# x loaded ahead of everything by tile, constants made early, passes on the identity before x is scaled, and a split signal in the sample rounds

## The reference

```
h = rms_norm(x) * norm1_w
z = h @ w_in                          # B, C, X of a short convolution, q, k, v, memory q, three gates
Y_A = W_convout(B * conv3(C * X))     # branch A
Y_B = differential attention          # 8 heads; the samples attend to 2048 cached keys and values each
Y_C = cross attention into memory     # 4 heads, 256 memory rows
x = x + W_o(sum_b sigmoid(G_b h) * Y_b)
x = x + PEER(rms_norm(x))             # 8 heads, top 16 of 16384 experts, gathered rows of peer_u and peer_v
```

## Time and profile before

| | us |
|---|---|
| median of 3 runs | 2830.64 (2829.07 to 2833.45) |
| the profiled execution | 2829.35 |
| its span | 2827.7 |

### The profile page before, as it was taken

One profiled execution on the slowest core, in us unless ns is written; L12 is line 12 of the kernel. 1 busy time (PEld: TensorE's weight loads), 2 busy tenths in 40 slices (PEclk: granted clock), 3 DMA queues, 4 the chain that ended last, 5 costly groups with the idle time before them and its releaser, 6 DMA issues.

```text
span 2827.7 us, 28082 instructions
## 1 busy us (share of the span) xinstructions
PE 2469.4 (87%) x9129; PEld 1588.6 (56%) x9129; DVE 1412.7 (50%) x2187; ACT 353.0 (12%) x759; POOL 1043.9 (37%) x952
## 2 busy tenths in 40 slices
PE   7999999999999999999998777777999497777777
PEld 5788888878766678888776323322333143233333
DVE  2365566973322223000167687786554656555543
ACT  2111000003221210000211111110111011111010
POOL 1065566120122210000026655656535454555542
PEclk9999999999999999999999899999899899999999
DMA  4398999695699975443379999999999989999998
GB/s 147 130 335 315 319 352 345 199 327 196 245 345 333 330 257 181 134 147 120 119 280 351 419 415 422 417 413 411 422 421 413 417 362 421 421 421 417 414 421 371
DMA packets 305394, 913.68 MB, mean 323 GB/s; under 512 B 15634, under 2 KB 195946, under 8 KB 236652
## 3 DMA queue, kind: packets, MB, share of 16 engines
q0 software_dynamic: 122304, 723.48, 63.8%
q1 hardware_dynamic: 182980, 188.92, 20.4%
HBM read 905.80 MB, written 6.56 MB: 323 GB/s over the span
## 4 chain that ended last, share of the span: by engine, by line
PE 54%; DMA 23%; DVE 12%; issue 4%; POOL 4%; ACT 2%; DVEq 0%; POOLq 0%; ACTq 0%; SPq 0%
PE ps L578 21%; PE ps L656 11%; DMA sb_S<-in_peer_u_dram,sb_ring 9%; PE ps L884 7%; DMA sb_bregion<-in_peer_u_dram,sb_ring 6%; PE ps L668 5%; DMA sb_mkv<-in_peer_u_dram,sb_ring 3%; PE ps L646 3%; PE ps L758 2%; DVE sb_bregion L1770 2%; DMA sb_S<-in_peer_v_dram,sb_ring 1%; DVE sb_S L1770 1%; DMA sb_wring<-in_peer_v_dram,sb_ring 1%; POOL sb_bregion L487 1%; DMA sb_wring<-in_w_in_dram 1%
## 5 line engine op out<-in xcount | busy, mean ns | idle before, releaser
L884 PE MATMUL ps<-sb_wring,sb_ring 128*128 128x512 f32 x992 | 464.0, 619 | 127.1 <-DMA sb_wring<-in_peer_v_dram,sb_ring 75.9
L578 PE MATMUL ps<-sb_hT,sb_wring 128*128 128x264 f32 x2304 | 530.7, 392 | 14.8 <-DMA sb_wring<-in_w_peer_q_dram 7.7
L578 PEld LDWEIGHTS ps<-sb_hT,sb_wring 128*128 128x128 f32 x2304 | 440.8, 193 | 96.9 <-issue 20.2
L884 PEld LDWEIGHTS ps<-sb_wring,sb_ring 128*128 128x128 f32 x992 | 189.6, 197 | 401.3 <-issue 265.9
L1770 DVE CUSTOM_DVE_ANT_0 sb_bregion<-sb_bregion,sb_rows 128x2048 f32<-128x2048 f32 x128 | 293.7, 2295 | 230.3 <-DMA sb_bregion<-in_peer_u_dram,sb_ring 223.2
L656 PE MATMUL ps<-sb_hT,sb_wring 128*128 128x264 f32 x1536 | 366.4, 389 | 1.9 <-DVEq L1185 1.6
L656 PEld LDWEIGHTS ps<-sb_hT,sb_wring 128*128 128x128 f32 x1536 | 287.7, 190 | 65.4 <-issue 16.4
L487 POOL DMA_INDIRECT sb_bregion<-in_peer_u_dram,sb_ring x132 | 190.0, 1440 | 280.0 <-DVEq L1185 225.5
L884 PE MATMUL ps<-sb_hT,sb_ring 128*128 128x512 f32 x496 | 231.3, 615 | 48.2 <-DMA sb_hT<-in_peer_v_dram,sb_ring 37.2
L884 PE MATMUL ps<-sb_oreg,sb_ring 128*128 128x512 f32 x496 | 227.7, 606 | 39.9 <-DMA sb_oreg<-in_peer_v_dram,sb_ring 36.1
L1152 ACT ACTIVATE sb_ring<-sb_ident,sb_ring 128x128 f32<-128x128 f32 x248 | 99.6, 402 | 912.3 <-PE ps L884 709.0
(11 more groups left out here) (350 smaller groups left out, 2539.9 us busy)
## 6 DMA issues: line engine op xcount, KB each, us to landing
sb_wring<-in_w_in_dram SPq DMA_DIRECT2D x52, 2048.0 KB
sb_ring<-in_cache_k_dram POOLq DMA_DIRECT2D x64, 512.0 KB, 6.2
sb_mkv<-in_cache_k_dram POOLq DMA_DIRECT2D x64, 512.0 KB, 6.5
sb_mkv<-in_cache_v_dram POOLq DMA_DIRECT2D x48, 512.0 KB, 7.0
sb_rows<-in_cache_v_dram POOLq DMA_DIRECT2D x47, 512.0 KB, 6.7
sb_wring<-in_w_mem_kv_dram SPq DMA_DIRECT2D x8, 2048.0 KB
sb_wring<-in_w_o_dram SPq DMA_DIRECT2D x8, 2048.0 KB
sb_wring<-in_w_peer_q_dram SPq DMA_DIRECT2D x8, 2048.0 KB
```

The source lines that it names most:

```text
L578: last = mm(ps[:, (2 * r + c) % 4, 0:NT], wring[:, r, k, c * P:(c + 1) * P], rhs[:, k, :], start=(k == 0), stop=(k == KC - 1))
L884: last = mm(ps[:, 4 * t + q, :], diag[:, k % 4, :], e_slots[v % ER][:, q * 512:(q + 1) * 512], start=False, stop=q_stop, skip_group_check= ...
```

## The change

- SP loads x first, in three DMAs with a semaphore each: tile 0 (`x_in`), tile 1 (`x_in1`), the samples (`x_in2`). The four small loads follow, then the weights.
- POOL makes `ident` and `ones` first. Its 12 loads then wait for tiles 0 and 1 of x.
- TensorE waits for `consts` and runs nine matmuls of the identity against `ones`, 512 columns each, into a bank that nothing reads; after the transpose of `colrows` it runs four more.
- ACT runs one element of Square before it waits for x, and one of Sqrt after its sum of squares (each brings its function table).
- x is scaled in place, tile 0 by DVE and tile 1 by ACT, and then transposed on the identity; only the 8 sample rows keep the matmul with a diagonal. `cols_ready` is waited for at k = 7, not ahead of k = 0. The transposes of the state, and DVE's copy of them, move behind the sixteen k.
- DVE copies the state rows and runs `own_maxima` ahead of the last turn of the memory loop.
- `turn_maxima`, `spread_maxima` and `sum_partitions` move within `aside` by 2 to 4 matmuls.
- `mask_sums` signals `sums_masked` after the multiplication; a new signal `sums_added` follows the sum over heads, and `columns` waits for that.

```diff
+            sp.dma_start(x_rows[:, 0, :], A["x_prompt"][0, 0:P, :]).then_inc(s["x_in"], 16)
+            sp.dma_start(x_rows[:, 1, :], A["x_prompt"][0, P:2 * P, :]).then_inc(s["x_in1"], 16)
+            sp.dma_start(x_rows[0:TS, 2, :], A["x_sample"].rearrange("b t d -> (b t) d")).then_inc(s["x_in2"], 16)
             sp.dma_start(colrows[0:16, :], A["norm1_w"][0].rearrange("(k p) -> k p", p=P)).then_inc(s["cols_in"], 16)
...
-            sp.dma_start(x_rows[:, 0:2, :], A["x_prompt"][0].rearrange("(t p) d -> p t d", p=P)).then_inc(s["x_in"], 16)
-            sp.dma_start(x_rows[0:TS, 2, :], A["x_sample"].rearrange("b t d -> (b t) d")).then_inc(s["x_in"], 16)
...
+            st(nc.gpsimd.memset(ones[:, :], 1.0))
+            pool.sem_inc(s["consts"], 1)
+
+            pool.wait_ge(s["x_in"], 16)
+            pool.wait_ge(s["x_in1"], 16)
...
+            def warm(n):
+                for _ in range(n):
+                    mm(ps[:, 5, :], ident[:, :], ones[:, :].unsqueeze(1).broadcast_to([P, 4, P]), start=True, stop=True)
             pe.wait_ge(s["consts"], 1)
+            warm(9)
             pe.wait_ge(s["cols_in"], 64)
-            nc.tensor.transpose(ps[:, 0, 0:72], colrows, ident[0:72, 0:72]).then_inc(s["cols_full"], 1)
-            pe.wait_ge(s["st_in"], 16)
...
+            nc.tensor.transpose(ps[:, 7, 0:72], colrows, ident[0:72, 0:72]).then_inc(s["cols_full"], 1)
+            warm(4)
...
-            pe.wait_ge(s["x_scaled"], 1)
+            pe.wait_ge(s["x_scaled"], 2)
...
-                for t, (first, n) in enumerate(TILES):
-                    last = mm(ps[:, k % 8, first:first + n], x_rows[0:n, t, k * P:(k + 1) * P], small[0:n, t, 0:n], start=True, stop=True)
-                last.then_inc(s["xT_full"], 1)
+                transpose_rows(x_rows, k, k % 8, TILES[0:2])
+                mm(ps[:, k % 8, TP:NT], x_rows[0:TS, 2, k * P:(k + 1) * P], small[0:TS, 2, 0:TS], start=True, stop=True).then_inc(s["xT_full"], 1)
...
-                pe.wait_ge(s["sums_masked"], m + 1)
+                pe.wait_ge(s["sums_added"], m + 1)
...
-                if (q, k) == (2, 7):
+                if (q, k) == (2, 11):
                     spread_maxima(0, nk)
-                if (q, k) == (3, 4):
+                if (q, k) == (3, 8):
                     sum_partitions(0, nk)
...
+            st(A_(stat[:, 61:62], stat[:, 61:62], ACT.Sqrt))
             root(1, stat[:, 0:3])
+            act.wait_ge(s["x_ss2"], 1)
+            st(A_(x_rows[:, 1, :], x_rows[:, 1, :], ACT.Copy, scale=stat[:, 1:2]))
+            act.sem_inc(s["x_scaled"], 1)
...
-            for t, (_, n) in enumerate(TILES):
-                st.run(TSC(small[0:n, t, 0:n], ident[0:n, 0:n], stat[0:n, t:t + 1], None, ALU.mult))
+            st.run(TSC(x_rows[:, 0, :], x_rows[:, 0, :], stat[:, 0:1], None, ALU.mult))
+            st.run(TSC(small[0:TS, 2, 0:TS], ident[0:TS, 0:TS], stat[0:TS, 2:3], None, ALU.mult))
...
-            with st.loop(TS // 2, 8) as i:
+            with st.loop(TS // 2 - 1, 8) as i:
+                score_memory(i)
             dve.wait_ge(s["cs_full"], 1)
             st(CP(cs_rows[0:2 + TS, :].rearrange("p (a b) -> p a b", a=2), ps[0:2 + TS, 6:8, :]))
             signal("cs_rows")
+            own_maxima()
+            score_memory(TS // 2 - 1)
...
+                signal("sums_masked")
                 st(RED(own_sum[:, 0:DC // heads], own_heads.rearrange("p (h c) -> p c h", h=heads), X, ALU.add))
-                signal("sums_masked")
+                signal("sums_added")
```

More of the change, by code:

```diff
@@ L567, in _ @@
                     pe.wait_ge(s[("xT_taken", "xT_taken2")[k % 2]], (k - 8) // 2 + 1)
-                for t, (first, n) in enumerate(TILES):
-                    last = mm(ps[:, k % 8, first:first + n], x_rows[0:n, t, k * P:(k + 1) * P], small[0:n, t, 0:n], start=True, stop=True)
-                last.then_inc(s["xT_full"], 1)
+                transpose_rows(x_rows, k, k % 8, TILES[0:2])
+                mm(ps[:, k % 8, TP:NT], x_rows[0:TS, 2, k * P:(k + 1) * P], small[0:TS, 2, 0:TS], start=True, stop=True).then_inc(s["xT_full"], 1)
             pe.wait_ge(s["xT_taken"], BC)
             pe.wait_ge(s["xT_taken2"], BC)
+            pe.wait_ge(s["st_in"], 16)
+            for j in range(BC):
+                last = nc.tensor.transpose(ps[:, 6, j * 16:(j + 1) * 16], ring4[0:16, 0, j * P:(j + 1) * P], ident[0:16, 0:16])
+            last.then_inc(s["st_full"], 1)
             def chunk(r, c, n, rhs):
@@ L1390, in _, with own_maxima, score_memory @@
             memory_key_norm()
-            with st.loop(TS // 2, 8) as i:
+            def own_maxima():
+                dve.wait_ge(s["self_full"], 1)
+                st(CP(b0, ps[:, 3, 0:P]))
+                st(TT(b1, b1, b0, ALU.max))
+                signal("max_full")
+            def score_memory(i):
                 for par in range(2):
@@ L1421, in _ @@
             over_m = lambda ap: ap[:, 0:n_m].rearrange("p (b h) -> p b h", b=TS).unsqueeze(2).broadcast_to([P, TS, 2, MH])
-            def own_maxima():
-                dve.wait_ge(s["self_full"], 1)
-                st(CP(b0, ps[:, 3, 0:P]))
-                st(TT(b1, b1, b0, ALU.max))
-                signal("max_full")
             def exponents():
@@ L1587, in _ @@
             st.settle()
-            own_maxima()
             first_merge(0)
```

37 lines of the change are left out of this document (17 added, 20 removed).

## The result

| | before | after |
|---|---|---|
| median, us (runs) | 2831.18 (2829.07 to 2833.45, 4) | 2807.94 (2801.87 to 2811.18, 4) |
| ratio, 95% interval | | 0.9914 (0.9901 to 0.9927) |
| profiled execution, span | 2829.35, 2827.7 | 2810.3, 2808.6 |

The changed kernel is 23 us faster by the medians and 19.1 us in the profiled executions. The forecast was 32.5 us and 2798, with 2806 as the upper end of its range: the direction was right, the size was not. Six more runs of the changed kernel beside the kernel before gave 2804.97 (2803.23 to 2813.63), ratio 0.9906 (0.9891 to 0.9922).

A forecast was written before the change was run, and what follows sets the result against it. TensorE was taken as the bound up to about 1400 us, then the expert gathers. Gains of 19.8 (start), 3.1 (maxima) and 9.6 (value rounds) sum to 32.5 us, for a median of 2798, range 2791 to 2806.

The follow-up runs named there:

- the diagonals behind passes: Changed kernel with x turned by matmuls on the three diagonals, as before the change, behind the same load and passes: 2806.28 us, ratio 0.9920; again 2801.67.
- both grouped forms: Changed kernel turning x in two halves, 16 transposes then 16 records of 8 columns: 2797.00 us; with three transposes a k in groups of four k: 2797.48 us.

## What to carry over

Price a mixed sequence of TensorE records from a row in which the same mix runs, not by adding the prices of parts from runs of one shape, and group records of one height where the order is free. Once TensorE is early, look at who was just in time behind it, here the weights of the next chunk. A range for one measured kernel must hold what its executions differ by in stages that the change doesn't touch, here some 10 us.

## What the runs showed of the hardware

- **Alternating heights cost more than the records.** 16 transposes of 128 rows took 1.89 us and 16 records of 8 rows 1.88 at the high clock; alternating two and two, a k cost 0.68 instead of 0.47. With the 8 rows transposed as well, 0.53 alternating and 0.34 in groups of four k; with matmuls on diagonals, 0.95 and 0.73.
- **Keeping the clock and bringing it are two things.** The 96 records on the diagonals ran 26.8 us at the low clock in before without bringing the high one, and kept it in all three profiles where the passes had raised it (through 15.25 us in two, through 11.8 in the one with groups of four k). The clock of before rose at 53.1, 4 us into the first chunk. The window of before shows 17 records in 4 us and that of the diagonals behind passes 26, both with 1.00 in the column of the clock:

```profile
35.00:39.00 4.00, 4.00 (x17) 3.28 (x15) 0.58 (x2) 0.48 (x1) 0.00 (x0) 1.00 0.02 4
```

```profile
20.00:24.00 4.00, 4.00 (x26) 3.44 (x26) 0.98 (x2) 0.96 (x2) 0.00 (x0) 1.00 0.78 125
```

- So ahead of the first change that it records, the column's 1.00 is no reading; the pace of the records is. From there on it agreed with the pace in the stretches read here.
- **Transposes held a raised clock in part of the executions**: in two of three profiles with three in a row, for 8.4 us, and in both grouped forms (7.6 and 5.5 us; one of them has small matmuls in it); in the third it fell after 2 us. At h2 it held in three of eighteen profiles. The mix of transposes and records of 8 columns lost it after 3.4 to 4.7 us in three of three. What decides it in a single execution is open.
